# The squares of eight norms added elementwise before the products of ones, and the second mixer's query norms moved into its softmax, on one Trainium2 core

## The reference

```python
def rms_norm(x, gain):
    xf = x.astype(jnp.float32)
    y = xf * lax.rsqrt(jnp.mean(xf * xf, axis=-1, keepdims=True) + RMS_EPS)
    return (y * gain.astype(jnp.float32)).astype(x.dtype)
...
    q = rms_norm(q, q_gain)
    k = rms_norm(k, k_gain)
...
    logits = jnp.einsum('bcqhgd,bckhd->bhgcqk', qc, kw).astype(jnp.float32) * (HEAD_DIM ** -0.5)
    logits = logits - slopes[None, :, :, None, None, None] * dist
...
    probs = jax.nn.softmax(jnp.concatenate([logits, sink], axis=-1), axis=-1)[..., :-1]
```

## Time and profile before

| | |
|---|---|
| median of 3 runs | 1953.47 us (1952.23 to 1953.7) |
| profiled execution, its time | 1953.21 us |
| its span, first to last instruction | 1951.4 us |
| mean granted clock of PE | 0.987 of full speed |

### The profile page before, as it was taken

The page is one execution under the profiler, slowest core; times in us unless marked ns, Lnnn a source line. Parts: engine busy times, 40 slices in busy tenths (PEclk is TensorE's granted clock), DMA queues, the critical chain, the costliest instruction groups (busy, mean ns, idle before and its releaser), DMA issues.

```text
span 1951.4 us, 29326 instructions
## 1 busy us (share of the span) xinstructions
PE 1793.9 (92%) x11292; PEld 1432.7 (73%) x11292; DVE 1288.2 (66%) x2375; ACT 917.3 (47%) x1897; POOL 297.5 (15%) x323
## 2 busy tenths in 40 slices
PE   8999999999999999999999888999978777787777
PEld 8999988999999999689999778995423222232222
DVE  5556886666665575976555857877677776766454
ACT  5444555444544453754444436643544344344333
POOL 2000001000000000010001000224433333333331
PEclk9999999999999999999999889999999999999999
DMA  7555425965555545135554423579999999999997
GB/s 287 194 177 183 143 89 150 267 241 178 164 191 194 191 134 178 43 109 184 194 181 144 140 87 122 177 268 400 405 422 421 421 421 422 421 422 421 421 422 316
DMA packets 96138, 485.02 MB, mean 249 GB/s; under 512 B 10576, under 2 KB 10832, under 8 KB 62976
## 3 DMA queue, kind: packets, MB, share of 16 engines
q0 software_dynamic: 38544, 275.25, 36.5%
q1 hardware_dynamic: 57456, 207.90, 32.1%
HBM read 478.65 MB, written 4.46 MB: 248 GB/s over the span
## 4 chain that ended last, share of the span: by engine, by line
PE 62%; DMA 13%; issue 9%; DVE 8%; POOL 5%; ACT 3%; POOLq 0%; SPq 0%; ACTq 0%; DVEq 0%
PE PS L541 16%; PE PS L542 16%; PE PS L543 16%; PE PS L2180 4%; DMA raw<-uv,A 3%; DMA WH<-uv,A 2%; PE PS L2201 2%; DMA YH<-uv,A 2%; DMA XF<-uv,A 2%; DMA WL<-uv,A 2%; DVE WL L1021 2%; PE PS L1655 1%; POOL raw L641 1%; DMA XH<-uv,A 1%; DMA YL<-uv,A 1%
## 5 line engine op out<-in xcount | busy, mean ns | idle before, releaser
L1021 DVE TENSOR_TENSOR WL<-raw,WH 128x1024 fp32r<-128x1024 f32 (+1 forms) x375 | 447.6, 1234 | 88.7 <-ACT WH L658 88.3
L541 PE MATMUL PS<-XH,WH 128*128 128x256 f32 x1616 | 462.8, 286 | 12.2 <-DVE A L1408 4.4
L542 PE MATMUL PS<-XL,WH 128*128 128x256 f32 x1616 | 458.4, 284 | 0.0
L543 PE MATMUL PS<-XH,WL 128*128 128x256 f32 x1616 | 457.9, 283 | 0.0
L658 ACT ACTIVATE WH<-raw 128x1024 fp32r<-128x1024 f32 (+1 forms) x375 | 371.0, 1040 | 38.8 <-PE PS L543 17.4
L541 PEld LDWEIGHTS PS<-XH,WH 128*128 128x128 f32 x1616 | 308.4, 191 | 17.2 <-DVE A L1408 5.7
L542 PEld LDWEIGHTS PS<-XL,WH 128*128 128x128 f32 x1616 | 308.6, 191 | 0.2
L543 PEld LDWEIGHTS PS<-XH,WL 128*128 128x128 f32 x1616 | 308.6, 191 | 0.0
L964 ACT ACTIVATE A<-A,RTK 128x1 f32<-128x1 f32 x256 | 75.0, 293 | 298.7 <-DVE A L1611 297.2
L541 PE MATMUL PS<-GH,WH 128*128 128x256 f32 x704 | 198.1, 281 | 0.0
L542 PE MATMUL PS<-GL,WH 128*128 128x256 f32 x704 | 197.8, 281 | 0.0
(11 more groups left out here) (309 smaller groups left out, 2990.8 us busy)
## 6 DMA issues: line engine op xcount, KB each, us to landing
raw<-wst SPq DMA_DIRECT2D x381, 512.0 KB, 4.6
raw<-wst SPq DMA_DIRECT2D x8, 384.0 KB, 3.4
vscr<-A POOLq DMA_DIRECT2D x1, 3072.0 KB, 37.1
A<-vscr POOLq DMA_DIRECT2D x1, 2048.0 KB, 22.2
C<-cst SPq DMA_DIRECT2D x1, 1236.5 KB, 10.7
raw<-uv,A POOLq DMA_INDIRECT x65, 19.6
hT<-xin SPq DMA_DIRECT2D x2, 512.0 KB, 5.0
A<-vscr POOLq DMA_DIRECT2D x1, 1024.0 KB, 12.7
```

Source lines behind the costliest of these rows:

```text
L541: pe.matmul(o, wh, xh, start=start, stop=False, skip_group_check=True)
L542: pe.matmul(o, wh, xl, start=False, stop=False, skip_group_check=True)
L543: return pe.matmul(o, wl, xh, start=False, stop=stop, skip_group_check=True)
L1021: dv.tensor_tensor(WL[:, m % SPL, 0:w], raw[:, i % RAW, 0:w], f32(WH[:, m % SPL, 0:w]), ALU.subtract).then_inc(s_lo, 1)
```

## The change

For p = 1, 3, 4 and 6 ACT squares between its scaled copies and DVE adds neighbours (`pairs`), so that PE multiplies four sums with ones; p = 6 adds XF likewise. For p = 2, 5 and 7 POOL adds each square to the first and PE multiplies one. p = 0 stays. The queries are no longer normed: their squares are added per token (a product with two columns of `bones`, tokens on the partitions), the root SR scales the slope of the bias (SL), and its reciprocal RQ scales the exponential and the maximum; both gains go to the keys (GQK). The projections use banks 0, 1, 6, 2, 3 and 4, and the turned root and the squares' products stand later.

```diff
-        RS = E1[:, 0:1280].rearrange("p (a b) -> p a b", a=5)
+        RS = E1[:, 0:T]
+
+        SR, RQ, SL = (A[:, 16512 + 16 * n:16528 + 16 * n].rearrange("p (t b e) -> p t b e", t=4, b=2) for n in range(3))
+        GQK = small[:, 60:61]
         M2 = E1[:, 0:1536].rearrange("p (n a t) -> p n a t", n=3, a=2)
...
+        IN_PAIRS = (1, 3, 4, 6)
+        SQ0 = [sum(8 if q in (0, 6) else 4 if q in IN_PAIRS else 1 for q in range(p)) for p in range(9)]
...
-                    po.tensor_tensor(SQ[:, kc, :], hT[:, kc, :], hT[:, kc, :], ALU.mult).then_inc(s_sq, 1)
+                    ins = po.tensor_tensor(SQ[:, kc, :], hT[:, kc, :], hT[:, kc, :], ALU.mult)
+                    if p == 0:
+                        ins.then_inc(s_sq, 1)
+                    elif kc == 0:
+                        own(ins)
+                    else:
+                        own(ins)
+                        own.wait()
+                        ins = po.tensor_tensor(SQ[:, 0, :], SQ[:, 0, :], SQ[:, kc, :], ALU.add)
+                        if kc < 7:
+                            own(ins)
+                if p:
+                    ins.then_inc(s_sq, 1)
...
-            squares(6)
...
+                squared = 0
...
                     high_x(p, kc)
-                if p in (1, 3, 4):
-                    ac.wait_ge(s_sums, p)
-                    for kc in range(8):
-                        ac.activation(SQ[:, kc, :], hT[:, kc, :], ACT.Square).then_inc(s_sq, 1)
+
+                    while p in IN_PAIRS and squared < (0, 0, 0, 2, 2, 4, 4, 8)[kc]:
+                        if squared == 0:
+                            ac.wait_ge(s_sums, p)
+                        ac.activation(SQ[:, squared, :], hT[:, squared, :], ACT.Square).then_inc(s_sqr, 1)
+                        squared += 1
...
             for t in range(4):
                 hi("qa", t)
-                if t == 0:
-                    root(6)
-                    ac.wait_ge(s_lt, 2)
-                    ac.activation(RT[:, 1, :], RT[:, 1, :], ACT.Sqrt, bias=c("eps", 0, 1), scale=1.0 / D).then_inc(s_lta, 1)
+            root(6)
+            ac.wait_ge(s_lt, 2)
+            ac.activation(RT[:, 1, :], RT[:, 1, :], ACT.Sqrt, bias=c("eps", 0, 1), scale=1.0 / D).then_inc(s_lta, 1)
...
-            ac.activation(RS[:, 4, :], PS[:, 4, 0:T], ACT.Sqrt, bias=c("eps", 0, 1), scale=1.0 / 64).then_inc(s_qrs, 1)
-            ac.activation(RS[:, 0:4, :], PS[:, 2:4, :].rearrange("p a (b t) -> p (a b) t", b=2), ACT.Sqrt,
-                          bias=c("eps", 1, 2), scale=1.0).then_inc(s_qrs, 1)
+            ac.activation(RS, PS[:, 2, 0:T], ACT.Sqrt, bias=c("eps", 0, 1), scale=1.0 / 64).then_inc(s_qrs, 1)
+            ac.activation(SR.rearrange("p t b e -> p (t b e)"), PS[:, 0, 0:16], ACT.Sqrt, bias=c("eps", 1, 2), scale=1.0).then_inc(s_qrs, 1)
...
+                            ex = ac.activation(sl, sl, ACT.Exp, bias=stats[:, 0, i % 3, e, b:b + 1], scale=RQ[:, i, b, e:e + 1],
                                                accum_out=stats[:, 1, i % 3, e, b:b + 1])
...
+            def pairs(p):
+
+                for i in range(4):
+                    dv.wait_ge(s_sqr, 8 * IN_PAIRS.index(p) + 2 * i + 2)
+                    dv.tensor_tensor(SQ[:, 2 * i, :], SQ[:, 2 * i, :], SQ[:, 2 * i + 1, :], ALU.add).then_inc(s_sq, 1)
...
+                pairs(p)
...
+            for i in range(4):
+                dv.wait_ge(s_xfq, 2 * i + 2)
+                dv.tensor_tensor(XF[:, 2 * i, :], XF[:, 2 * i, :], XF[:, 2 * i + 1, :], ALU.add).then_inc(s_sq, 1)
+            for t in range(4):
+                lo("qa", t)
+            dv.wait_ge(s_rt, 7)
+            own(dv.reciprocal(RT[:, 0, :], RT[:, 0, :]))
+            own.wait()
...
+            dv.wait_ge(s_rstd, 7)
             for t in range(5):
-                lo(*(("qa", t) if t < 4 else ("ka", 0)))
-                if t == 0:
-                    dv.wait_ge(s_rt, 7)
-                    own(dv.reciprocal(RT[:, 0, :], RT[:, 0, :]))
-                    own.wait()
...
                 dv.wait_ge(s_used, U("qa", t) if t < 4 else U("ka", 0))
-                dv.scalar_tensor_tensor(out=QA[:, t, :], in0=PS[:, (0, 1, 6, 7, 0)[t], 0:T], scalar=1.0, in1=RT[:, 1, :],
+                dv.scalar_tensor_tensor(out=QA[:, t, :], in0=PS[:, (0, 1, 6, 2, 3)[t], 0:T], scalar=1.0, in1=RT[:, 1, :],
                                         op0=ALU.mult, op1=ALU.mult).then_inc(s_qa, 1)
-                if t == 3:
-                    by_token(1)
-
-            def qk_norm(t):
-                own(dv.reciprocal(RS[:, t, :], RS[:, t, :]))
-                own.wait()
-                dv.scalar_tensor_tensor(out=QA[:, t, :], in0=QA[:, t, :], scalar=c("sgain", t // 4, t // 4 + 1), in1=RS[:, t, :],
-                                        op0=ALU.mult, op1=ALU.mult).then_inc(s_qk, 1)
-
+            lo("ka", 0)
+            by_token(1)
...
+            lo("va", 0)
             dv.wait_ge(s_qrs, 1)
-            qk_norm(4)
-            lo("va", 0)
+            own(dv.reciprocal(RS, RS))
+            own.wait()
+            dv.scalar_tensor_tensor(out=QA[:, 4, :], in0=QA[:, 4, :], scalar=GQK, in1=RS, op0=ALU.mult, op1=ALU.mult).then_inc(s_qk, 1)
             lo("vb", 0)
             dv.wait_ge(s_qrs, 2)
-            qk_norm(0)
+            dv.reciprocal(RQ.rearrange("p t b e -> p (t b e)"), SR.rearrange("p t b e -> p (t b e)"))
+            dv.tensor_tensor(SL, SR, c("slope").rearrange("p (t e) -> p t e", t=4).unsqueeze(2).broadcast_to([128, 4, 2, 2]),
+                             ALU.mult).then_inc(s_qk, 1)
...
             ins.then_inc(s_vb, 1)
-            qk_norm(2)
-            qk_norm(3)
...
+                dv.wait_ge(s_qk, 2)
                 for e in range(2):
-                    ins = dv.scalar_tensor_tensor(out=st[:, e, :], in0=c("dist"), scalar=c("slope", 2 * j + e, 2 * j + e + 1),
-                                                  in1=ps[:, e, :], op0=ALU.mult, op1=ALU.add)
+                    for b in range(2):
+                        k = slice(128 * b, 128 + 256 * b)
+                        ins = dv.scalar_tensor_tensor(out=st[:, e, k], in0=c("dist", k.start, k.stop), scalar=SL[:, j, b, e:e + 1],
+                                                      in1=ps[:, e, k], op0=ALU.mult, op1=ALU.add)
...
+                own.wait()
+                own(dv.tensor_tensor(nm, nm, RQ[:, j].rearrange("p b e -> p e b"), ALU.mult))
...
-                for kc in range(8):
-                    pe.wait_ge(s_sq, 8 * p + kc + 1)
-                    ins = pe.matmul(PS[:, 7, 0:T], c("ones"), SQ[:, kc, :], start=kc == 0, stop=kc == 7, skip_group_check=True)
+                n = 8 if p == 0 else 4 if p in IN_PAIRS else 1
+                for i in range(n):
+                    pe.wait_ge(s_sq, SQ0[p] + i + 1)
+                    ins = pe.matmul(PS[:, 7, 0:T], c("ones"), SQ[:, i if n == 8 else 2 * i, :], start=i == 0, stop=i == n - 1, skip_group_check=True)
                 if p == 6:
-                    for kc in range(8):
-                        pe.wait_ge(s_xfq, kc + 1)
-                        ins = pe.matmul(PS[:, 7, T:2 * T], c("ones"), XF[:, kc, :], start=kc == 0, stop=kc == 7,
+                    for i in range(4):
+                        pe.wait_ge(s_sq, SQ0[6] + 4 + i + 1)
+                        ins = pe.matmul(PS[:, 7, T:2 * T], c("ones"), XF[:, 2 * i, :], start=i == 0, stop=i == 3,
...
-            for t in range(2, 5):
-                if t == 3:
-                    pe.wait_ge(s_lt, 1)
-                if t == 4:
-                    pe.wait_ge(s_qa, 1)
-                gemm(*(("qa", t) if t < 4 else ("ka", 0)), 0, 8, X, PS[:, (0, 1, 6, 7, 0)[t], 0:T]).then_inc(s_used, 1)
-                if t == 2:
-                    sums(6)
-                if t == 3:
-                    by_token(6)
-            pe.wait_ge(s_qa, 2)
-            gemm("va", 0, 0, 8, X, PS[:, 1, 0:T]).then_inc(s_used, 1)
-            for t in range(5):
-                pe.wait_ge(s_qaq, t + 1)
-                ins = pe.matmul(PS[:, (2, 2, 3, 3, 4)[t], (t % 2) * T if t < 4 else 0:(t % 2) * T + T if t < 4 else T],
-                                c("bones"), SQ[:, t, :], start=True, stop=True, skip_group_check=True)
-            ins.then_inc(s_qas, 1)
+            gemm("qa", 2, 0, 8, X, PS[:, 6, 0:T]).then_inc(s_used, 1)
+            sums(6)
+            gemm("qa", 3, 0, 8, X, PS[:, 2, 0:T]).then_inc(s_used, 1)
+            gemm("ka", 0, 0, 8, X, PS[:, 3, 0:T]).then_inc(s_used, 1)
+            gemm("va", 0, 0, 8, X, PS[:, 4, 0:T]).then_inc(s_used, 1)
+            by_token(6)
+
+            def square_sums():
+
+                for t in range(4):
+                    pe.wait_ge(s_qaq, t + 1)
+                    for blk in range(2):
+                        pe.matmul(PS[:, 0, 4 * t + 2 * blk:4 * t + 2 * blk + 2], SQ[:, t, 128 * blk:128 * blk + 128],
+                                  c("bones")[:, 0:128:64], start=True, stop=True, skip_group_check=True)
+                pe.wait_ge(s_qaq, 5)
```

(49 more changed lines are left out.)

21 lines of the change are left out of this document (8 added, 13 removed).

## The result

The changed kernel takes 1939.76 us (median of four, 1937.4 to 1941.29) against 1952.85 for the kernel before (1950.37 to 1953.7): a ratio of 0.9934, 95% interval 0.9917 to 0.9951, or 13.1 us less. Forecast were 1944.6, 8.6 less.

The account below looks back on a forecast made before the run. TensorE, busy 92% of the span, was taken to bound the kernel. Terms -4.8 + 7.2 - 2.5 - 1.0 - 7.5 gave -8.6 us, 1944.6 us; own range 1940 to 1949, eight in ten 1939.5 to 1953.

Parts of the forecast that it names:

- p = 1, 3, 4: Three norms going from eight products of ones to four: 1.6 us saved each, -4.8 together, bounds -5.2 and -3.3.
- p = 2: Norm where POOL comes late: each sum waits for its square, PE idles and its clock drops; +7.2 us.
- p = 5: Norm going from eight products to one: 3.0 us saved, less 0.4 for a late weight; -2.5, bounds -3.0 and 0.
- p = 6 and second mixer: Third query projection through softmax: a new weight wait, then fewer root waits and query norms; -7.5 us, bounds -4 and -11.
- p = 7 and gathers: Last norm, eight products to one, ahead of the row gathers: -1.0 us, bounds -2.5 and +1.9.
- the likeliest case: At the second mixer's preceding late POOL norm near 325: dependent steps of 1.24 us, costing +7.2 us together.
- no stall: Rival at POOL's late norm near 325: sums hide behind squares, term about 0.5, whole 1937.9 us; chance 0.06.
- 3.0 us a step: Rival of a dear POOL chain near 325, deciding from this step cost; 1958.3 us at 3.2; chance 0.10 with other PE stalls.
- The upper bound: For POOL's late norm near 325: +9.6 us, if each wait on POOL were 0.2 us dearer.
- the rival: POOL's sums each block DVE's subtraction for 0.8 us at two norms; 1952.4 us; chance 0.22, shared with a weaker second mixer.
- the new wait: Ahead of the third query projection: PE waits 3.9 us for a weight whose subtraction stands behind DVE's sums.
- One sign of being wrong: In the second mixer's softmax: fillings after the third still waiting as long as now would make the norms' removal worthless.

Follow-up runs that it names:

- the two later chips: The changed kernel unaltered, measured again on two other chips against the kernel before: 1949.43 us, 0.997, and 1946.96 us, 0.996.
- the mixer alone: The kernel before with only the second mixer's part of the change, all norms' squares as before with eight products each: 1942.96 us, 0.9952.

## Why the prediction was right, and where it was off

By the first measurement the range held it, if by 0.3 us: 1939.76 against a lower end of 1939.5, and just below the forecast's own 1940 to 1949. The direction and two thirds of the size came as said. On the two later chips the time lies well inside, but by a stop that the prediction knew nothing of; that is luck. Term by term, from the two first traces, whose spans differ by 15.8:

```
term                      predicted   measured   what it is measured by
p = 1, 3, 4               -4.8        -5.1       1.71, 1.73 and, without a dip of the clock, 1.69
p = 2                     +7.2        +8.1       9.57 of wait, 3.87 of products saved, 2.4 of half clock (1.6 to 2.7 in others)
p = 5                     -2.5        -2.8       sums to third query projection; with eight: 3.0
p = 6 and second mixer    -7.5        -7.7       -10.3 in the traces, 2.6 of it a dip of before; -6.4 to -8.9 with others
p = 7 and gathers         -1.0        -4.0       gather phase 662.5 to 658.5; p = 7 with eight: 3.8
dips of the clock                     -4.2       near 760 (1.55) and 1137 (2.6); the start, 0.1 more
```

**p = 2** came as the likeliest case said, with its step 1.37 us instead of 1.24, so 0.9 more of wait: not the wait on the semaphore was dear (0.07 to 0.08 between the rows) but the sum, 0.72 where a square takes 0.61. The rivals "no stall" and "3.0 us a step" are both out. The upper bound was summed wrongly: seven waits at 0.2 us are 1.4 on 7.2, 8.6 and not 9.6.

**p = 5** and POOL against DVE: POOL's sum stretches from 0.72 alone to 1.60 us beside DVE, and DVE's subtraction stays at the 1.63 that it had beside a square. Timelines of POOL and DVE:

```profile
860.32 0.79 POOL L598 TENSOR_TENSOR A<-hT 128x256 f32<-128x256 f32 x1
861.19 1.60 POOL L606 TENSOR_TENSOR A<-A 128x256 f32<-128x256 f32 x1
...
860.02 0.62 DVE L1048 SCALAR_TENSOR_TENSOR XL<-hT,C,XH 128x256 fp32r<-128x256 f32 x1
860.56 1.63 DVE L1040 TENSOR_TENSOR WL<-raw,WH 128x1024 fp32r<-128x1024 f32 x1
```

A block takes 2.44 us instead of 2.28, so DVE loses 0.16 a block, in the low copy (0.62 instead of 0.47), not the 0.8 of the rival nor the 0.34 with which the prediction reckoned and for which no row stands. The Trainium skill, SBUF — State Buffer, section Who interferes with whom, speaks of an exclusive lock between the two, in which the order of issue decides who waits. The trace agrees, and the order is what the prediction left out: the sum starts at 861.19, when the subtraction has run since 860.56, and ends 0.60 us after it, about what a sum takes alone, so it reads as the sum waiting for the subtraction; the 0.41 that the subtraction loses fits the rest of the square that had started ahead of it. POOL had the time: its last sum ends at 869.29, 2.1 us ahead of PE. Where DVE had no work of POOL beside it before, as in the kernel with p = 2's chain moved ahead, the price is the larger one, 2.44 a block instead of some 1.9.

**p = 6 and the mixer**: the new wait was 3.52 us (3.9 said), its half clock cost 1.4 (1.7 said). The first release came 7.9 us closer to the start of the mixer; the 9.0 of the prediction leaves that half clock out, and with it out the measured figure is 9.3. That the order on DVE made that wait is shown by moving it. What of the gain belongs to the banks and what to the norms was not run apart; in the two traces the way from the third query projection to the first scores is 3.4 us shorter (35.17 for 38.56), and from there to the first release, where two norms of DVE went, 4.5 (9.95 for 14.49; 4.3 said). One sign of being wrong was a bad one: PE's waits from the third filling on are as long as before (1.83, 3.07, 2.24 and 3.57 us became 2.20, 3.43, 2.24 and 3.58), and the gain made ahead of them stays all the same, 9.3 us for the mixer alone.

**p = 7 is the term that was mis-sized.** The step that failed is "I take 1.5 of 3.0 back there, and 0.5 lost by the same POOL and DVE conflict": all 3.0 us came back, and some 0.6 to 1.0 more, as holes of 4 us in the gathers' rate closed; why 3.0 us of PE become 3.6 to 4.0 of gathers was not taken further. The bound of -2.5 was too tight as well. The conflict cost nothing there: from the sums of p = 6 to those of p = 7 the second trace of the changed kernel takes 200.93 us and the kernel with eight products at p = 7 201.00, and the first gather stands 10.27 us behind the start of the sums, before 10.24.

Last, the prediction took the profiled execution of before as it was. Half clock near 760, without any wait of PE ahead of it, was in it, and it is in nine of the fourteen traces; so was one behind a wait of 3.07 us in the mixer, which all but the first trace of the changed kernel have. So one pair of traces shows 15.8 where the medians show 13.1.

## What to carry to other kernels

Folding eight products into one by sums on a slow engine pays only where that engine has time ahead of the product: here the same edit was worth -2.8 us at one norm and +8.1 at another, where the engine's program came late to it. Placing it earlier took the stall away, but the medians did not fall below those with eight products: there the sums slowed another engine. When work moves to an engine that also makes weights ready, put it behind the weight that is needed next. Work on TensorE ahead of a transfer-bound stage may be a cover for another engine's lateness, which is not shown here but fits the traces; measure on more than one chip before calling its removal a gain.

## What the runs showed of the hardware, unexpected

The granted clock fell to half without a wait of PE ahead of it: from 715 to 779 us no trace has a wait of PE above 0.1 us. Windows of 760 to 764, the kernel before, first and second trace of the changed one (columns as above; 0.62 and 0.72 are a mean over stretches at 1.2 and 2.4 GHz):

```profile
760.00:764.00 4.00, 4.00 (x23) 3.81 (x22) 2.68 (x4) 0.00 (x0) 0.00 (x0) 0.62 0.15 27
```

```profile
760.00:764.00 4.00, 4.00 (x36) 4.00 (x36) 1.81 (x3) 0.00 (x0) 0.00 (x0) 1.00 0.11 46
```

```profile
760.00:764.00 4.00, 4.00 (x28) 4.00 (x28) 2.06 (x4) 0.00 (x0) 0.00 (x0) 0.72 0.11 41
```

The dip comes in nine of the fourteen traces between 752 and 768 and costs 1.5 us; the same program has it in one execution and not in another. From the wait of 3.4 us near 1137 to the next wait the first trace of the changed kernel took 17.1 us at full clock, all others 18.5 to 19.8 with a half clock in it. That wait in the first trace, with the clock of the stretch behind it, and the same stretch of before:

```profile
1136.64 0.66 PE L1772 MATMUL PS<-A 128*64 128x256 f32 x4 [3.43 <-DVE YL L1114]
...
1136.00:1154.00 18.00, 14.71 (x120) 13.67 (x121) 12.52 (x29) 5.43 (x8) 0.00 (x0) 1.00 0.39 118
```

```profile
1146.00:1166.00 20.00, 17.21 (x119) 15.78 (x120) 11.92 (x27) 5.42 (x8) 0.00 (x0) 0.84 0.32 106
```

A wait does not always bring the lower clock, then, and the lower clock does not always come from a wait. A difference of 2 us between two single traces of this kernel shows nothing until the clock's rows have been compared.
